# Rows beyond an expert's 96: blocks of 96 against blocks of 32, column-tiled and with the next block's transfers begun early

## The chip, the cores and the metric

One core of a Trainium2 chip runs the whole program in one launch. The metric is the device time of one launch in microseconds (us), as the median of three runs. TensorE, VectorE, ScalarE, GpSimd and SyncE are written PE, DVE, ACT, POOL and SP, as in the profile; a q behind the name (SPq, PEldq) is the engine's own sequencer with its branches, register operations and DMA issues.

## What is computed

The program is a small diffusion-like network (a gMLP layer, an RWKV layer, two attention layers) on 512 tokens and 256 context tokens of width 1024. Both of its first two layers end in a mixture of experts, which is where the change lies:

```python
def hier_moe(h, w_grp, b_grp, w_exp, b_exp, w_gate, w_up, w_down):
    ...
    expert_id = (grp[:, None] * EXPERTS_PER_GROUP + top_idx).reshape(-1)
    ...
    def expert_block(args):
        xb, e = args
        return (jax.nn.silu(xb @ w_gate[e]) * (xb @ w_up[e])) @ w_down[e]
    ...
    return jnp.einsum('tk,tkd->td', weights, y)
```

Each token is sent to 2 of 32 experts. In layer 0 there are 768 tokens (1536 rows over all experts), in layer 1 there are 512 (1024 rows). An expert has a gate and an up matrix of 1024 by 512 and a down matrix of 512 by 1024, all float32: 2 MB each, 6 MB an expert. Nothing bounds how many rows one expert gets. With the inputs that the reference draws, its router gives 114, 101 and 120 rows to the three busiest experts of layer 0 and 97 to the busiest of layer 1; all others have at most 96.

## The kernel before

`moe` runs five parts one after the other for each of the two layers: `norm_turn` (normalises the tokens, stores them in `h_rows`, and begins the loads of experts 0 and 1), `route`, `experts`, `experts_beyond`, `combine`. Each part is a block of its own, and all engines meet at its end; the helper `signals` then clears the semaphores in a short block of its own (L42, L46).

`route` works out on DVE which expert each row goes to and which place it has there. The first 96 rows (`CAP`) of an expert sit in the expert's own cell; rows above that go to further cells of 96. `index` holds for each cell the tokens of its rows, `home` for each token the rows of its results, `beyond` the number of further cells and the expert that owns each. All tables are as wide as the largest possible number of further cells, `blocks_beyond(nt)`: 16 in layer 0 and 10 in layer 1. L787 to L795 compare each count and place with the multiples of 96, L807 and L809 build the tables over all cells, L736 multiplies them on PE, L816 copies out the index.

`experts` goes through the 32 experts in a fixed, unrolled order. Weights sit in a ring of two (`wgu`, `wd`): SP fetches those of expert e+2 as soon as the sums of expert e are done. Each 96 rows are worked as 3 groups of 32; with 32 rows only a quarter of PE's columns is filled, so four quarters of the output columns are computed side by side on four column tiles (L886 gate and up, L904 down). Results leave in four stores by POOL (L866).

`experts_beyond` is a loop in hardware (`Fori`, L999) over all possible further cells, with an `If` (L1000) whose body runs for the cells that exist. A body is a block by itself:

```python
sp.dma_start(wgu[:, 0, 0, :, :], gate_src[bass.ds(e, 1)].rearrange("a p k f -> p (a k) f")).then_inc(gate_in, 16)
...
pool.indirect_dma_start(xs[:, :], None, h_rows, bass.IndirectOffsetOnAxis(ap=lanes[:, 0:1].bitcast(U32), axis=0)).then_inc(x_in, 16)
...
sp.wait_ge(y_ready, 2)
...
sp.wait_ge(y_out, 16)
```

SP issues gate, up and down weights (L1007 to L1009), POOL copies the cell's column of the index (L1016) and gathers the rows (L1018); PE turns them (L1024), multiplies all 96 rows at once with 512 columns (L1030), turns the hidden rows (L1034) and multiplies by the down matrix (L1040). DVE moves the turned rows (L1052) and the results (L1060), ACT applies silu (L1046). SP stores the results and waits until they have landed (L1011); then the block ends, the semaphores are cleared and the next turn of the loop begins.

`combine` gathers the two results of each token (L1086, POOL), loads the gate rows (L1078, SP) and adds into `x` on DVE (L1095 to L1098).

Of the kernel before, what the change touches and what calls it, by code (L numbers as in the profile page):

```python
# [7 lines left out]
P = 128  # L8
# [81 lines left out]
def constants():  # L90

    i, j = np.meshgrid(np.arange(P), np.arange(P), indexing="ij")
    return side_by_side({"ident": i == j, "before": i < j, "ones": np.ones((P, P)), "iota": np.tile(np.arange(P), (P, 1)),
                         "caps": np.tile(CAP * np.arange(1, 9), (P, 1)), "tokens": i[:, :NTA] + P * j[:, :NTA]})
# [26 lines left out]
def blocks_beyond(nt):  # L121

    return (2 * nt * P) // CAP
# [7 lines left out]
class Core:  # L131


    def __init__(self, nc, held, ins):
# [8 lines left out]
        self.y_rows = nc.dram_tensor("y_rows", [(E + blocks_beyond(NTA)) * CAP, D], F32, kind="Internal").ap()  # L143
# [500 lines left out]
def moe(core, layer, nt):  # L644
# [3 lines left out]
    nb = E + blocks_beyond(nt)  # L648
    with ExitStack() as held:
# [9 lines left out]
        beyond = sb("blocks_beyond", [P, blocks_beyond(nt) + 1], I32)  # L659
# [5 lines left out]
        gate_in, gate_in1, up_in, up_in1, down_in, down_in1, router_in, kept0, kept1 = held.enter_context(  # L665
            signals(nc, "gate_in0 gate_in1 up_in0 up_in1 down_in0 down_in1 router_in kept0 kept1"))
# [18 lines left out]
        experts(core, layer, h_rows, y_rows, index, wgu, wd, gate_src, up_src, down_src, gate_in, up_in, down_in)  # L685
        experts_beyond(core, layer, nt, h_rows, y_rows, index, beyond, wgu, wd, gate_src, up_src, down_src)
        combine(core, layer, nt, y_rows, weights, home)


def route(core, layer, nt, nb, br, kept, weights, index, home, beyond):  # L690
# [3 lines left out]
    more = -(-nt * P // CAP) - 1  # L694
    with ExitStack() as held:
# [17 lines left out]
        owner = sb("owner", [P, nbb, E])  # L713
# [6 lines left out]
        with nc.Block() as block:  # L720
# [26 lines left out]
            def _(dve):  # L747
# [49 lines left out]
                dve.tensor_scalar(first, blk, 1.0, None, ALU.min)  # L797
                do(dve.scalar_tensor_tensor(shift, shift, float(E - 1), iota[:, 0:E], ALU.add, ALU.subtract))
                dve.scalar_tensor_tensor(row, blk, float(-CAP), where, ALU.mult, ALU.add)
# [1960 lines left out]
```

## Time and profile before

| | |
|---|---|
| median of 3 runs | 4519.39 us (4518.64 to 4523.71) |
| the profiled execution | 4529.52 us, its span 4527.7 us |
| PE busy | 3775.3 us (83% of the span) |
| DVE, ACT, POOL busy | 1255.0, 777.2, 617.6 us |
| mean transfer rate | 154 GB/s |

The shares are means over very different stages. `experts` of layer 0 runs from about 747 to 1357 us, that of layer 1 from about 2969 to 3579 us; each is followed by `experts_beyond` and `combine`. "us" in a row is the start or the busy time as its view says; a row with three numbers and slashes gives the shortest, the median and the longest in ns.

### The profile page before, as it was taken

To read this page: it belongs to the slowest core of one execution; us is meant where nothing else is said; L and a number is where in the kernel's file an instruction comes from. 1 tells how busy PE (TensorE), PEld (TensorE's weight loads), DVE (VectorE), ACT (ScalarE), POOL (GpSimd) and SP (SyncE) were. 2 spreads that over 40 slices of the span, in tenths; PEclk is the share of its full clock that TensorE was granted. 3 is DMA by queue.
4 is the path that set the end of the run, shared out by engine and by line. 5 is a ranking of instruction groups with operands and counts; after the bars stand their busy time and mean duration, and the time that the engine had idled before them with its cause. 6 is when DMAs were issued, how large, how long until landed. Compare 5 with 4: busy or idle time off the path is not lost. (4 is left out here: it accounts for less than half of the span.)

```text
span 4527.7 us, 102783 instructions
## 1 busy us (share of the span) xinstructions
PE 3775.3 (83%) x45908; PEld 2400.6 (53%) x45908; DVE 1255.0 (28%) x2935; ACT 777.2 (17%) x1775; POOL 617.6 (14%) x792
## 2 busy tenths in 40 slices
PE   4999986999985289878888887789999739997787
PEld 2455535555552135467777775445555414564464
DVE  2140123111110530055545554421111120232153
ACT  1011001000000100133433331100000010231142
POOL 0000000111110100054444441011111010000000
PEclk7999996999997589889999997789999869758999
DMA  7731106999985332100000002279999633101100
GB/s 280 281 140 37 70 30 238 381 381 375 372 303 184 108 86 85 59 14 20 27 17 17 17 6 101 103 287 380 379 371 375 225 104 101 57 1 48 37 38 24
DMA packets 297853, 697.12 MB, mean 154 GB/s; under 512 B 26509, under 2 KB 49517, under 8 KB 296780
## 3 DMA queue, kind: packets, MB, share of 16 engines
q1 hardware_dynamic: 263268, 602.54, 37.0%
q0 software_dynamic: 26192, 73.25, 5.0%
q10 hardware_dynamic: 7960, 14.81, 0.9%
q8 instruction: 363, 5.95, 0.5%
q14 instruction: 70, 0.57, 0.0%
HBM read 636.40 MB, written 54.14 MB: 153 GB/s over the span
## 5 line engine op out<-in xcount | busy, mean ns | idle before, releaser
L886 PE MATMUL banks<-w_gate_up_ring,x_turned 128*32 128x256 f32 x12288 | 700.8, 384 | 63.5 <-DMA w_gate_up_ring<-in_moe_w_up_dram 62.0
L886 PEld LDWEIGHTS banks<-w_gate_up_ring,x_turned 128*32 128x32 f32 x12288 | 435.6, 111 | 302.7 <-issue 94.4
L904 PE MATMUL banks<-w_down_ring,hidden_turned 128*32 128x256 f32 x6144 | 344.8, 380 | 0.0
L962 DVE TENSOR_TENSOR hidden<-silu_gate,banks 128x128 f32<-128x128 f32 x192 | 55.3, 288 | 807.1 <-ACT silu_gate L942 807.1
L866 POOL DMA_DIRECT2D y_rows<-y_out_rows x256 | 141.0, 559 | 986.6 <-ACT y_out_rows L948 949.5
L904 PEld LDWEIGHTS banks<-w_down_ring,hidden_turned 128*32 128x32 f32 x6144 | 193.7, 110 | 128.0 <-issue 0.2
L337 PE MATMUL banks<-const_cols,h_tokens 128*128 128x128 f32 x240 | 55.0, 409 | 214.7 <-DVE h_tokens L310 143.6
L1883 DVE TENSOR_TENSOR inverse_both_ways<-banks,inverse_both_ways 128x512 f32<-128x512 f32 (+1 forms) x240 | 152.2, 637 | 255.3 <-PE banks L1792 254.4
L854 POOL DMA_INDIRECT x_rows<-h_rows,cell_index x64 | 62.7, 979 | 919.8 <-POOLq L42 893.6
L456 PE MATMUL banks<-gmlp_weights,h_turned_gmlp 128*128 128x512 f32 x384 | 173.3, 606 | 13.1 <-DMA gmlp_weights<-in_ga_w_in_dram 13.1
L1781 PE MATMUL banks<-inverse_both_ways,l_quarters 64*64 64x64 f32 x3840 | 150.7, 225 | 29.6 <-POOL inverse_both_ways L1965 21.7
L942 ACT ACTIVATE silu_gate<-banks 128x128 f32<-128x128 f32 x192 | 53.3, 278 | 711.0 <-PE banks L886 711.0
L630 PE MATMUL banks<-gmlp_weights,u_channels 128*128 128x512 f32 x384 | 165.1, 592 | 0.8 <-DVE u_channels L596 0.8
L487 PE MATMUL banks<-h_turned_gmlp,gmlp_weights 128*128 128x384 f32 x512 | 165.3, 486 | 0.0
L1300 PE MATMUL banks<-mixed,proj_weights 128*128 128x384 f32 x512 | 165.3, 486 | 0.0
L337 PEld LDWEIGHTS banks<-const_cols,h_tokens 128*128 128x128 f32 x240 | 45.7, 217 | 225.1 <-DVE h_tokens L310 151.6
L1781 PEld LDWEIGHTS banks<-inverse_both_ways,l_quarters 64*64 64x64 f32 x3840 | 130.7, 138 | 54.8 <-POOL inverse_both_ways L1965 24.6
L1792 PE MATMUL banks<-inverse_both_ways,step 64*64 64x64 f32 x3840 | 153.4, 220 | 0.3
L1911 ACT ACTIVATE step<-banks 128x256 f32<-128x256 f32 x240 | 92.2, 384 | 270.3 <-PE banks L1781 264.9
L1792 PEld LDWEIGHTS banks<-inverse_both_ways,step 64*64 64x64 f32 x3840 | 133.2, 137 | 3.2 <-ACT step L1911 2.6
L1300 PEld LDWEIGHTS banks<-mixed,proj_weights 128*128 128x128 f32 x512 | 97.3, 190 | 68.1 <-issue 0.5
L1970 POOL TENSOR_TENSOR l_quarters<-l_and_rb,scan_masks 128x256 f32<-128x256 f32 x192 | 123.5, 666 | 72.0 <-PE banks L1781 71.7
(452 smaller groups left out, 5530.1 us busy)
## 6 DMA issues: line engine op xcount, KB each, us to landing
w_gate_up_ring<-in_moe_w_gate_dram SPq DMA_DIRECT2D x68, 2048.0 KB, 20.7
w_gate_up_ring<-in_moe_w_up_dram SPq DMA_DIRECT2D x68, 2048.0 KB, 25.0
w_down_ring<-in_moe_w_down_dram SPq DMA_DIRECT2D x68, 2048.0 KB, 22.6
u_channels<-in_ada_w_dram SPq DMA_DIRECT2D x40, 1024.0 KB, 7.0
y_rows<-y_out_rows POOLq DMA_DIRECT2D x256, 96.0 KB, 5.4
gmlp_weights<-in_ga_w_in_dram SPq DMA_DIRECT2D x8, 2048.0 KB, 8.1
ab_weights<-in_ab_w_in_dram SPq DMA_DIRECT2D x6, 2048.0 KB, 8.6
ada_first<-in_ada_w_dram SPq DMA_DIRECT2D x2, 4096.0 KB, 18.3
```

The costliest lines, as they stand in the source:

```text
L337: last = pe.transpose(core.ps[:, 2 * (j % 2) + half, k * P:(k + 1) * P], h[:, j % 2, c0:c0 + P], core.c("ident"))
L456: last = pe.matmul(core.ps[:, step % 6, :], hT[:, k, t * P:(t + 1) * P], wring[:, i % 2, k, :], start=k == 0, stop=k == KD - 1)
L487: last = pe.matmul(core.ps[:, (step + 2) % 8, 0:TOK], wring[:, i % 2, k, m * P:(m + 1) * P], hT[:, k, half * TOK:(half + 1) * TOK], start= ...
L630: last = pe.matmul(core.ps[:, bank, :], uT[:, rest * KD + k, t * P:(t + 1) * P], wring[:, rest, k, :], start=rest == 0 and k == 0, stop=re ...
L866: pool.dma_start(y_blocks[e, j], ys[strip(j), r, :, :]).then_inc(y_out[r], 16)
L886: last = pe.matmul(ps[strip(j), GU + g, 0:2 * FQ].rearrange("p (a c) -> p a c", a=2), xT[:, e % 2, k, strip(g)], wgu[:, e % 2, :, k, j * F ...
L904: last = pe.matmul(ps[strip(j), Y + g // 2, (g % 2) * DQ:(g % 2 + 1) * DQ], hT[:, g, strip(k)], wd[:, e % 2, k, j * DQ:(j + 1) * DQ], star ...
L1300: last = pe.matmul(ps[:, i % 8, 0:HT2], wring[:, n % 2, k, m * P:(m + 1) * P], mix[:, j % 2, k, half * HT2:(half + 1) * HT2], start=k == 0 ...
L1781: last = pe.matmul(ps[row[cc], 4 * h + 1, u * CHUNK:(u + 1) * CHUNK], LQ[h][row[cc], n % 2, u, :], XX[h][row[cc], 0, u, :], start=True, st ...
L1792: last = pe.matmul(ps[row[cc], 4 * h, (4 + u) * CHUNK:(5 + u) * CHUNK], Z[h][row[cc], u, :], XX[h][row[cc], 1, u, :], start=True, stop=True)
L1883: DVE.mark(dve.tensor_tensor(x, ps[:, 4 * h, at], x, ALU.add), by_dve, f"XX{n}_{h}")
L1970: POOL.mark(pool.tensor_tensor(by_dir(LQ[h][:, n % 2, :, :]), by_dir(LR[h][:, :, 0, :]), quarters(n), ALU.mult), by_pool, f"LQ{n}_{h}")
```

## The change

- Rows beyond an expert's 96 are put in cells of 32 instead of 96. `blocks_beyond` becomes 2 * ceil((tokens - 96) / 32): 42 in layer 0 and 26 in layer 1, and the tables of `route` grow with it. `route` has three small DVE operations more, for places and result rows in cells of two sizes.
- A body of the loop now works 32 rows on four column tiles, as `experts` does: 32 products for gate and up together, one turn of the hidden rows, 16 products for down.
- The first further cell's rows and weights are fetched in `experts`: weights behind those of the last expert, the gather behind the stores of expert 30, into a tile of its own (`xb`). Each body then fetches the next cell's rows once its own are turned, and the next cell's weights once its own sums are done, into the same half of the ring. The semaphores of these loads (`next_gu`, `next_d`) live across bodies; SP passes them on to the body's own.
- The last body also begins a load, which no one uses; `combine` waits for it on SP.
- The results leave in four stores on ACT's queue instead of one on SP's, and ACT waits for them.

```diff
@@ -120,7 +120,7 @@
 
 def blocks_beyond(nt):
 
-    return (2 * nt * P) // CAP
+    return 2 * -(-(nt * P - CAP) // ROWS)
 
 
...
     tl = nt * P
-    nb = E + blocks_beyond(nt)
+    nb = E + blocks_beyond(nt) + 1
     with ExitStack() as held:
...
+        xb = sb("x_rows_beyond", [ROWS, D])
         gate_src = ins["moe_w_gate"][layer].rearrange("e (k p) f -> e p k f", p=P)
...
-            signals(nc, "gate_in0 gate_in1 up_in0 up_in1 down_in0 down_in1 router_in kept0 kept1"))
+        gate_in, gate_in1, up_in, up_in1, down_in, down_in1, router_in, kept0, kept1, next_gu, next_d = held.enter_context(
+            signals(nc, "gate_in0 gate_in1 up_in0 up_in1 down_in0 down_in1 router_in kept0 kept1 next_gu next_d"))
         gate_in, up_in, down_in = [gate_in, gate_in1], [up_in, up_in1], [down_in, down_in1]
 
         def loads(sp):
...
         lane_hot = sb("lane_hot", [P, 2 * nt, CAP])
         token_at = sb("token_at", [P, 2 * nt, nb])
-        owner = sb("owner", [P, nbb, E])
+        owner = sb("owner", [P, nbb + 1, E])
+        owners = sb("owners", [P, nbb + 1])
+        back = sb("rows_back", [P, 2 * nt])
...
                 dve.tensor_reduce(blk, past[:, :, :], AX, ALU.add)
                 do(dve.tensor_tensor(shift, whole, extra, ALU.subtract))
                 dve.tensor_scalar(first, blk, 1.0, None, ALU.min)
+                dve.scalar_tensor_tensor(row, blk, float(-ROWS), where, ALU.mult, ALU.add)
                 do(dve.scalar_tensor_tensor(shift, shift, float(E - 1), iota[:, 0:E], ALU.add, ALU.subtract))
-                dve.scalar_tensor_tensor(row, blk, float(-CAP), where, ALU.mult, ALU.add)
+                dve.scalar_tensor_tensor(row, first, float(ROWS - CAP), row, ALU.mult, ALU.add)
                 do(dve.tensor_tensor(work[:, :, :, :], one_hot[:, :, :, :], shift.unsqueeze(1).unsqueeze(1).to_broadcast([P, 2, nt, E]), ALU.mult))
                 do(dve.tensor_reduce(moved, work[:, :, :, :].rearrange("p a t e -> p (a t) e"), AX, ALU.add))
...
                 for n in range(2 * nt):
                     last = dve.tensor_scalar(token_at[:, n, :], iota[:, 0:nb], got[:, n:n + 1], tokens[:, n % nt:n % nt + 1], ALU.is_equal, ALU.mult)
                 last.then_inc(spread, 1)
-                dve.tensor_tensor(owner[:, :, :], whole.unsqueeze(1).to_broadcast([P, nbb, E]), iota[:, 0:nbb].unsqueeze(2).to_broadcast([P, nbb, E]), ALU.is_le)
+                dve.tensor_tensor(owner[:, :, :], whole.unsqueeze(1).to_broadcast([P, nbb + 1, E]), iota[:, 0:nbb + 1].unsqueeze(2).to_broadcast([P, nbb + 1, E]), ALU.is_le)
+                dve.scalar_tensor_tensor(back[:, :], got, float(-E), first, ALU.add, ALU.mult)
+                dve.tensor_copy(beyond[:, 0:1], whole[:, E - 1:E])
                 do(dve.scalar_tensor_tensor(row, got, float(CAP), row, ALU.mult, ALU.add))
+                dve.tensor_reduce(owners[:, :], owner[:, :, :], AX, ALU.add)
+                do(dve.scalar_tensor_tensor(row, back[:, :], float(ROWS - CAP), row, ALU.mult, ALU.add))
                 dve.tensor_copy(flat(home[:, :, :]), row)
-                dve.tensor_copy(beyond[:, 0:1], whole[:, E - 1:E])
-                do(dve.tensor_reduce(count[:, 3, 0:nbb], owner[:, :, :], AX, ALU.add))
-                dve.tensor_scalar(beyond[:, 1:nbb + 1], count[:, 3, 0:nbb], float(E - 1), None, ALU.min)
+                dve.tensor_scalar(beyond[:, 1:nbb + 2], owners[:, :], float(E - 1), None, ALU.min)
                 dve.wait_ge(tabled, 1)
                 dve.tensor_copy(index[:, :], core.ps[0:CAP, 2, 0:nb])
 
 
-def experts(core, layer, h_rows, y_rows, index, wgu, wd, gate_src, up_src, down_src, gate_in, up_in, down_in):
+def experts(core, layer, h_rows, y_rows, index, wgu, wd, gate_src, up_src, down_src, gate_in, up_in, down_in, beyond, xb, next_gu, next_d):
 
     nc = core.nc
     ps = core.ps
     X_LOW, X_HIGH, GU, H, Y = 0, 1, 2, 5, 6
...
@@ -847,6 +853,12 @@
                     sp.dma_start(wgu[:, r, 1, :, :], up_src[e]).then_inc(up_in[r], 16)
                     sp.wait_ge(y_sum, 2 * (e - 1))
                     sp.dma_start(wd[:, r, :, :], down_src[e]).then_inc(down_in[r], 16)
+                first = sp.value_load(beyond[0:1, 1:2], min_val=0, max_val=E - 1)
+                sp.wait_ge(gu_sum, GROUPS * (E - 1))
+                sp.dma_start(wgu[:, 0, 0, :, :], gate_src[bass.ds(first, 1)].rearrange("a p k f -> p (a k) f")).then_inc(next_gu, 16)
+                sp.dma_start(wgu[:, 0, 1, :, :], up_src[bass.ds(first, 1)].rearrange("a p k f -> p (a k) f")).then_inc(next_gu, 16)
+                sp.wait_ge(y_sum, 2 * (E - 1))
+                sp.dma_start(wd[:, 0, :, :], down_src[bass.ds(first, 1)].rearrange("a p k f -> p (a k) f")).then_inc(next_d, 16)
 
             @block.gpsimd
             def _(pool):
...
+                        pool.indirect_dma_start(xb[:, :], None, h_rows, bass.IndirectOffsetOnAxis(ap=index[0:ROWS, E:E + 1].bitcast(U32), axis=0)).then_inc(x_beyond, 16)
                 for r in range(2):
                     pool.wait_ge(y_out[r], 16 * QUARTERS * E // 2)
+                pool.wait_ge(x_beyond, 16)
 
             @block.tensor
             def _(pe):
...
-def experts_beyond(core, layer, nt, h_rows, y_rows, index, beyond, wgu, wd, gate_src, up_src, down_src):
+def experts_beyond(core, layer, nt, h_rows, y_rows, index, beyond, xb, next_gu, next_d, wgu, wd, gate_src, up_src, down_src):
...
+    X, GU, H, Y = 0, 1, 2, 3
+    QUARTERS = P // ROWS
+    FQ, DQ = F // QUARTERS, D // QUARTERS
+    strip = lambda j: slice(ROWS * j, ROWS * (j + 1))
+    y_blocks = y_rows[E * CAP:, :].rearrange("(b l) (q c) -> q l b c", l=ROWS, q=QUARTERS)
...
+        lanes = sb("lanes", [ROWS, 1], I32)
+        xT = sb("x_turned", [P, KD, ROWS])
+        sg = sb("silu_gate", [P, FQ])
+        h = sb("hidden", [P, FQ])
+        hT = sb("hidden_turned", [P, P])
+        ys = sb("y_out_rows", [P, DQ])
...
+        def block_beyond(b):
+            with signals(nc, "lanes_set x_in gu_here d_here x_turned x_moved gu_sum silu_done h_ready h_turned hT_ready y_sum y_ready y_stored", core.soft) as (
+                    lanes_set, x_in, gu_here, d_here, x_turned, x_moved, gu_sum, silu_done, h_ready, h_turned, hT_ready, y_sum, y_ready, y_stored):
+                with nc.Block() as block:
+                    @block.sync
+                    def _(sp):
+                        e = sp.value_load(beyond[0:1, bass.ds(b + 2, 1)], min_val=0, max_val=E - 1)
+                        sp.wait_ge(next_gu, 32)
+                        sp.sem_clear(next_gu)
+                        sp.sem_inc(gu_here, 1)
+                        sp.wait_ge(next_d, 16)
+                        sp.sem_clear(next_d)
+                        sp.sem_inc(d_here, 1)
+                        sp.wait_ge(gu_sum, 1)
+                        sp.dma_start(wgu[:, 0, 0, :, :], gate_src[bass.ds(e, 1)].rearrange("a p k f -> p (a k) f")).then_inc(next_gu, 16)
+                        sp.dma_start(wgu[:, 0, 1, :, :], up_src[bass.ds(e, 1)].rearrange("a p k f -> p (a k) f")).then_inc(next_gu, 16)
+                        sp.wait_ge(y_sum, 1)
+                        sp.dma_start(wd[:, 0, :, :], down_src[bass.ds(e, 1)].rearrange("a p k f -> p (a k) f")).then_inc(next_d, 16)
+
+                    @block.gpsimd
+                    def _(pool):
+                        pool.tensor_copy(lanes[:, :], index[0:ROWS, bass.ds(b + E + 1, 1)]).then_inc(lanes_set, 1)
+                        pool.wait_ge(lanes_set, 1)
+                        pool.wait_ge(x_turned, 1)
+                        pool.indirect_dma_start(xb[:, :], None, h_rows, bass.IndirectOffsetOnAxis(ap=lanes[:, 0:1].bitcast(U32), axis=0)).then_inc(x_in, 16)
+                        pool.wait_ge(x_in, 16)
+
+                    @block.tensor
+                    def _(pe):
+                        for k in range(KD):
+                            last = pe.transpose(ps[:, X, k * ROWS:(k + 1) * ROWS], xb[:, k * P:(k + 1) * P], core.c("ident", ROWS)[:, 0:ROWS])
+                        last.then_inc(x_turned, 1)
+                        pe.wait_ge(x_moved, 1)
+                        pe.wait_ge(gu_here, 1)
+                        for k in range(KD):
+                            for j in range(QUARTERS):
+                                last = pe.matmul(ps[strip(j), GU, 0:2 * FQ].rearrange("p (a c) -> p a c", a=2), xT[:, k, :],
+                                                 wgu[:, 0, :, k, j * FQ:(j + 1) * FQ], start=k == 0, stop=k == KD - 1)
+                        last.then_inc(gu_sum, 1)
+                        pe.wait_ge(h_ready, 1)
+                        pe.transpose(ps[:, H, 0:P], h[:, :], core.c("ident")).then_inc(h_turned, 1)
+                        pe.wait_ge(hT_ready, 1)
+                        pe.wait_ge(d_here, 1)
+                        for k in range(KF):
+                            for j in range(QUARTERS):
+                                last = pe.matmul(ps[strip(j), Y, 0:DQ], hT[:, strip(k)], wd[:, 0, k, j * DQ:(j + 1) * DQ], start=k == 0, stop=k == KF - 1)
+                        last.then_inc(y_sum, 1)
+
+                    @block.scalar
+                    def _(act):
+                        act.wait_ge(gu_sum, 1)
+                        act.activation(sg[:, :], ps[:, GU, 0:FQ], ACT.Silu).then_inc(silu_done, 1)
+                        act.wait_ge(y_ready, 1)
+                        for j in range(QUARTERS):
+                            act.dma_start(y_blocks[j][:, bass.ds(b, 1), :], ys[strip(j), :].unsqueeze(1)).then_inc(y_stored, 16)
+                        act.wait_ge(y_stored, 16 * QUARTERS)
+
+                    @block.vector
+                    def _(dve):
+                        dve.wait_ge(x_turned, 1)
+                        dve.tensor_copy(xT[:, :, :].rearrange("p k c -> p (k c)"), ps[:, X, 0:KD * ROWS]).then_inc(x_moved, 1)
+                        dve.wait_ge(silu_done, 1)
+                        dve.tensor_tensor(h[:, :], sg[:, :], ps[:, GU, FQ:2 * FQ], ALU.mult).then_inc(h_ready, 1)
+                        dve.wait_ge(h_turned, 1)
+                        dve.tensor_copy(hT[:, :], ps[:, H, 0:P]).then_inc(hT_ready, 1)
+                        dve.wait_ge(y_sum, 1)
+                        dve.tensor_copy(ys[:, :], ps[:, Y, 0:DQ]).then_inc(y_ready, 1)
+
         with nc.Fori(0, blocks_beyond(nt)) as b:
             with nc.If(left > b):
-                with signals(nc, "lanes_set x_in gate_in up_in down_in x_turned x_moved g_sum u_sum silu_done h_ready h_turned hT_ready y_sum y_ready y_out", core.soft) as (
...
+                block_beyond(b)
...
+                sp.wait_ge(next_gu, 32)
+                sp.wait_ge(next_d, 16)
```

## Rows read from the trace of the kernel before

**Rows 1.** Busy time by stretch: start and end, length, engines, granted clock, DMA share, GB/s.

```profile
811.00:1346.00 535.00, 500.58 (x8515) 310.65 (x8507) 77.15 (x229) 48.66 (x143) 88.64 (x140) 0.99 1.02 369
1361.70:1405.30 43.60, 25.70 (x60) 10.03 (x60) 3.63 (x6) 0.59 (x1) 1.16 (x2) 0.77 0.46 163
1489.00:1497.00 8.00, 0.00 (x0) 0.00 (x0) 0.00 (x0) 0.00 (x0) 0.24 (x1) 0.50 0.00 0
```

**Rows 2.** DMA issues: count, size, median us to landing.

```profile
y_rows<-y_out_rows_b SPq DMA_DIRECT2D x4, 384.0 KB, 3.0
```

**Rows 3.** Timeline of the three bodies of layer 0: start, us, engine, line, operation.

```profile
1352.53 2.16 POOL L866 DMA_DIRECT2D y_rows<-y_out_rows  x4 [15.22 <-ACT y_out_rows L948]
1361.72 0.18 POOL L1016 COPY lanes_b<-cell_index 96x1 int32 x1 [7.03 <-issue]
1362.81 0.40 SPq L1007 DMA_DIRECT2D w_gate_up_ring<-in_moe_w_gate_dram  x1
1370.39 1.54 PE L1024 MATMUL banks<-const_cols,x_rows_b 96*128 96x96 f32 x8 [18.89 <-DMA x_rows_b<-h_rows,lanes_b]
1373.79 16.50 PE L1030 MATMUL banks<-w_gate_up_ring,x_turned_b 128*96 128x512 f32 x32 [1.85 <-DMA w_gate_up_ring<-in_moe_w_gate_dram]
1392.34 7.11 PE L1040 MATMUL banks<-w_down_ring,hidden_turned_b 128*96 128x512 f32 x16 [0.65 <-DVE hidden_turned_b L1057]
1400.35 0.39 SPq L1011 DMA_DIRECT2D y_rows<-y_out_rows_b  x1
...
1405.33 0.18 POOL L1016 COPY lanes_b<-cell_index 96x1 int32 x1 [41.92 <-POOLq L42]
...
1485.71 0.37 SPq L1011 DMA_DIRECT2D y_rows<-y_out_rows_b  x1
```

**Rows 4.** Timeline of layer 1's only body and what follows.

```profile
3583.72 0.18 POOL L1016 COPY lanes_b<-cell_index 96x1 int32 x1 [6.97 <-POOLq L42]
...
3622.22 0.37 SPq L1011 DMA_DIRECT2D y_rows<-y_out_rows_b  x1
3631.34 0.83 SPq L1078 DMA_DIRECT2D gate_spread<-mods  x2
...
3640.20 0.75 DVE L1095 TENSOR_SCALAR y_back<-y_back,choice_weights 128x1024 f32<-128x1024 f32 x1 [18.15 <-DMA y_back<-y_rows,row_of_choice]
```

**Rows 5.** Timeline in `experts`: one group of 32 rows, then the down products of three.

```profile
1341.22 3.66 PE L886 MATMUL banks<-w_gate_up_ring,x_turned 128*32 128x256 f32 x64
...
1346.12 5.39 PE L904 MATMUL banks<-w_down_ring,hidden_turned 128*32 128x256 f32 x96
```

**Rows 6.** Landing after issue: up weights of L1008, then stores of L866.

```profile
DMA to landing us min/median/max: 15.0/15.5/16.7
...
DMA to landing us min/median/max: 2.1/5.4/7.2
```

**Rows 7.** Branches of the loop, L999, from the last body to `combine`: layer 0, then layer 1.

```profile
L999 SPq COMPARE_BRANCH  x27: 40/45/50, 1490.2 to 1498.7; - x27
L999 DVEq COMPARE_BRANCH  x27: 50/62/67, 1490.4 to 1499.8; - x27
L999 POOLq COMPARE_BRANCH  x27: 40/50/50, 1490.2 to 1496.0; - x27
L999 PEldq COMPARE_BRANCH  x27: 86/214/218, 1490.3 to 1500.0; - x27
L999 SPq COMPARE_BRANCH  x19: 40/50/60, 3626.7 to 3631.2; - x19
```

**Rows 8.** Timeline of the start of `combine` in layer 0.

```profile
1498.79 0.84 SPq L1078 DMA_DIRECT2D gate_spread<-mods  x2
1509.30 0.75 DVE L1095 TENSOR_SCALAR y_back<-y_back,choice_weights 128x1024 f32<-128x1024 f32 x1 [23.77 <-DMA gate_spread<-mods]
```

**Rows 9.** Timeline of `route` in layer 0: its tables.

```profile
739.98 0.68 DVE L809 TENSOR_TENSOR owner<-count,const_cols 128x512 f32<-128x512 f32 x1
744.22 0.20 DVE L816 CAST cell_index<-banks 96x48 int32<-96x48 f32 x1 [2.42 <-PE banks L736]
```

More of the change, by code:

```diff
@@ L93, in constants @@
     return side_by_side({"ident": i == j, "before": i < j, "ones": np.ones((P, P)), "iota": np.tile(np.arange(P), (P, 1)),
-                         "caps": np.tile(CAP * np.arange(1, 9), (P, 1)), "tokens": i[:, :NTA] + P * j[:, :NTA]})
+                         "caps": np.tile(CAP + ROWS * np.arange(21), (P, 1)), "tokens": i[:, :NTA] + P * j[:, :NTA]})
 def scan_constants():
@@ L658, in moe @@
         home = sb("row_of_choice", [P, 2, nt], U32)
-        beyond = sb("blocks_beyond", [P, blocks_beyond(nt) + 1], I32)
+        beyond = sb("blocks_beyond", [P, blocks_beyond(nt) + 2], I32)
+        xb = sb("x_rows_beyond", [ROWS, D])
         gate_src = ins["moe_w_gate"][layer].rearrange("e (k p) f -> e p k f", p=P)
@@ L684, in moe @@
         route(core, layer, nt, nb, br, [kept0, kept1], weights, index, home, beyond)
-        experts(core, layer, h_rows, y_rows, index, wgu, wd, gate_src, up_src, down_src, gate_in, up_in, down_in)
-        experts_beyond(core, layer, nt, h_rows, y_rows, index, beyond, wgu, wd, gate_src, up_src, down_src)
-        combine(core, layer, nt, y_rows, weights, home)
+        experts(core, layer, h_rows, y_rows, index, wgu, wd, gate_src, up_src, down_src, gate_in, up_in, down_in, beyond, xb, next_gu, next_d)
+        experts_beyond(core, layer, nt, h_rows, y_rows, index, beyond, xb, next_gu, next_d, wgu, wd, gate_src, up_src, down_src)
+        combine(core, layer, nt, y_rows, weights, home, next_gu, next_d)
 def route(core, layer, nt, nb, br, kept, weights, index, home, beyond):
@@ L693, in route @@
     nbb = blocks_beyond(nt)
-    more = -(-nt * P // CAP) - 1
+    more = nbb // 2
     with ExitStack() as held:
@@ L825, in experts @@
     FQ, DQ = F // QUARTERS, D // QUARTERS
-    y_blocks = y_rows.rearrange("(b g l) (q c) -> b q l g c", g=GROUPS, l=ROWS, q=QUARTERS)
+    y_blocks = y_rows[0:E * CAP, :].rearrange("(b g l) (q c) -> b q l g c", g=GROUPS, l=ROWS, q=QUARTERS)
     with ExitStack() as held:
@@ L834, in experts @@
         ys = sb("y_out_rows", [P, 2, GROUPS, DQ])
-        s = held.enter_context(signals(nc, "x_in0 x_in1 x_turned x_low x_high gu_sum silu_done h_ready h_turned hT_ready y_sum y_low y_high y_out0 y_out1", core.soft))
-        x_in0, x_in1, x_turned, x_low, x_high, gu_sum, silu_done, h_ready, h_turned, hT_ready, y_sum, y_low, y_high, y_out0, y_out1 = s
+        s = held.enter_context(signals(nc, "x_in0 x_in1 x_turned x_low x_high gu_sum silu_done h_ready h_turned hT_ready y_sum y_low y_high y_out0 y_out1 x_in", core.soft))
+        x_in0, x_in1, x_turned, x_low, x_high, gu_sum, silu_done, h_ready, h_turned, hT_ready, y_sum, y_low, y_high, y_out0, y_out1, x_beyond = s
         x_in, y_out = [x_in0, x_in1], [y_out0, y_out1]
@@ L989, in experts_beyond @@
     with ExitStack() as held:
         sb = lambda name, shape, dt=F32: held.enter_context(nc.sbuf_tensor(f"{name}_b{layer}", shape, dt))
-        lanes = sb("lanes", [CAP, 1], I32)
-        xs = sb("x_rows", [CAP, D])
-        xT = sb("x_turned", [P, KD, CAP])
-        sg = sb("silu_gate", [CAP, F])
-        h = sb("hidden", [CAP, F])
-        hT = sb("hidden_turned", [P, KF, CAP])
-        ys = sb("y_out_rows", [CAP, D])
-        left = nc.values_load(beyond[0:1, 0:1], min_val=0, max_val=blocks_beyond(nt))
+        lanes = sb("lanes", [ROWS, 1], I32)
@@ L1063, in combine @@
-def combine(core, layer, nt, y_rows, weights, home):
+                block_beyond(b)
+def combine(core, layer, nt, y_rows, weights, home, next_gu, next_d):
     nc = core.nc
```

59 lines of the change are left out of this document (2 added, 57 removed).

## The prediction

> **What bounds the kernel now.** I read the page's shares first (PE 83% busy, 154 GB/s on average) and then the busy time by stretch, because the mean says nothing about the stages that change. In `experts` PE runs at its upper clock level and the transfer engines are full, 369 GB/s [rows 1]: nothing is to be had there, and whatever is added to its traffic costs time. In a body of `experts_beyond` the picture is another: in 43.6 us PE is busy 25.7, the transfers run 46% of the time, one after the other [rows 1]. The count of result stores says how many bodies run: 4 in both layers together [rows 2]; the timeline puts three in layer 0 [rows 3] and one in layer 1 [rows 4].
>
> The timeline of a body shows why it is long. Weights are asked for at 1362.81, PE gets its rows at 1370.39 and its first weights at 1373.79; two products of 16.50 and 7.11 us follow; the store is issued at 1400.35 and the next body begins at 1405.33 [rows 3]. A store lands 3.0 us after its issue [rows 2], so 2.0 us of those 4.98 are the block's end, the clearing and the loop. Three bodies take from 1361.72 to the last landing at 1485.71 + 3.0 = 1488.7, 127.0 us; the one of layer 1 takes from 3583.72 to 3622.22 + 3.0 = 3625.2, 41.5 us.
>
> After the last body the loop goes on through its empty turns, 13 in layer 0 and 9 in layer 1. The branch rows give two branches a turn: SP (1498.7 - 1490.2) / 13 = 0.65 us, DVE 0.72, POOL 0.45, PE 0.75, and in layer 1 SP 4.5 / 9 = 0.50 [rows 7]. These turns are on the path: `combine` starts behind them.
>
> **How many bodies the new kernel runs.** Not the trace but the inputs decide this. The rows over 96 are 18, 5 and 24 in layer 0 and 1 in layer 1. Each is below 32, so three cells and one cell stay three and one.
>
> **A new body, step by step.** Let s be the moment when PE begins, about 0.3 us after POOL's copy of the index.
>
> 1. Rows are there already. Eight turns and one move of 256 columns. Before, eight turns of 96 rows took 1.54 us, and 3.4 us lay between their start and the first product, some of it a wait for weights [rows 3]. I take 1.8 (1.5 to 2.5).
> 2. Gate and up: 64 records, 3.66 us in `experts` [rows 5]. But PE has idled before, and the granted clock over a body is 0.77 against 0.99 [rows 1]. How much that costs: the 16 records of L1040 take 7.11 us, so 32 of L1030 would take 14.2 at the upper level, and took 16.50 [rows 3]. The 2.3 us lost mean some 4.6 us spent at 1.2 GHz instead of 2.4. Here that is most of the pass: 4.6 us do 2.3 us of work, the rest 1.4 us. That is 6.0, and 6.3 with the shorter warm-up before it (3.6 to 7.3). The sums are done at s + 8.1.
> 3. Silu, product, turn, move: between L1030's end and L1040's start lie 2.05 us with 512 columns [rows 3], in `experts` 1.24 between the last sums and the first down product, partly covered [rows 5]. I take 1.5.
> 4. Down: a third of 5.39 us [rows 5], 1.8 (to 3.6 at the lower level). s + 11.4.
> 5. Move of 256 columns 0.5; four issues on ACT: POOL's four took 2.16 us [rows 3], SP's single ones 0.39, so 2.0 (1.3 to 2.4).
> 6. Landing: stores that share the engines with weights took 2.1 to 7.2 us, 5.4 in the median [rows 6], those of the old body, alone, 3.0 [rows 2]. The next weights are in flight here, so 5.4. The results have landed at s + 19.3.
> 7. End, clearing, loop turn: 2.0 + 0.3. The next body begins at s + 21.6.
>
> The other bound of a body is the weights. SP can ask for the next 4 MB only at s + 8.1, because they go where the present ones lie. In the old body up landed 15.5 us after its issue, 16.4 after gate's, with down beside them [rows 6]; at the full 369 GB/s the 4.19 MB need 11.4. I take 14: they land at s + 22.3, and PE wants them at s + 21.6 + 1.8 = s + 23.4. That fits with 1 us to spare and fails by 1 us with 16.4, so I count 22 us from body to body. Down weights follow 6 us later and are wanted 8 us later. The gather is issued at about s + 1.5; before, 8.7 us lay between the copy of the index and PE's start on the gathered rows (1361.72 to 1370.39) [rows 3], so it arrives by s + 10 and is hidden by the same chain. SP waits inside its stream for the sums, but has nothing else behind them; ACT waits for its stores, with only the block's end behind.
>
> The first set of weights is asked for in `experts` one expert's time earlier than a body could. Before, the engines are idle for most of the last expert, so nothing there is delayed but the last four stores, issued at 1352.53 to 1354.7, whose landing may meet the last of 6 MB more. From there to the body lie 9.2 us [rows 3]. I add 1.5 us in each layer (0 to 3).
>
> Layer 0: two periods of 22 and 19.3 to the landing, 63.3 from s = 1362.0, so 1425.3 against 1488.7: -63.4. Layer 1: 3584.0 + 19.3 = 3603.3 against 3625.2: -21.9. Together -85.3, and +3 for the stores.
>
> **Empty turns.** There are 39 in layer 0 instead of 13, 25 in layer 1 instead of 9. Who comes to `combine` last matters. In layer 0 DVE began at 1509.30, when SP's gate rows had landed, 10.5 us after their issue and behind POOL's gathers [rows 8]; that is 19.2 us after the turns began. With 39 turns SP issues at 25.5; the gathers, begun at 39 x 0.45 = 17.4 plus 0.8, are then nearly over, so the gate rows land faster, within the 8.9 us that layer 1 shows for both kinds [rows 4]: 32 to 34 us, or +13 to +15. If SP's turn costs 0.50 as in layer 1, the gathers decide, +8. I take +11. In layer 1: 16 x 0.50 = +8 (7 to 10). Sum +19. PE's 39 x 0.75 = 29 us end inside `combine`, which has no work for it, and cost nothing. The unused load ends about 9 us after the last landing, before the gathers begin: nothing; if it were late, it would slow gathers that now take 8.9 us, by a few us at most.
>
> In the empty turns the transfer engines move nothing [rows 1], so this trace shows no instruction being fetched there. The Trainium skill, "Runtime: NRT & Kernel Launch", section "Instruction fetch mechanics", says that a taken branch whose target lies outside the fetched instructions waits for a fetch. That rule speaks against the change, which takes 42 more turns over a longer body; what it would do is the last rival below. The same skill's "Advanced Engine Details and Errata", section "Control Flow Timing", gives about 0.11 us for a compare-and-branch; by that an empty turn would be an estimated 0.2 us and the term +9 instead of +19. The rows decide for 0.45 to 0.75.
>
> **`route`.** Tables over 32 experts and the possible cells grow on DVE. L809 handles 512 elements in 0.68 us [rows 9], 1.3 ns each. Ahead of PE's product come 448 elements more in each of L787 and L790, 168 in each of L792 and L795, 324 in L807 and one operation: 2.2 us; in layer 1 776 elements and the operation, 1.2. The longer owner table (864 elements more, twice: 2.2 us) comes while DVE would wait 2.42 us for PE [rows 9]; without that wait it would cost those 2.2. I take +3 (2 to 6).
>
> **Sum.** -85.3 + 3 + 19 + 3 = -60.3. The terms come from the profiled execution, 4529.5 us with a span of 4527.7, 10 us above the median of 4519.4; stages this short scale by nothing worth counting. 4519.4 - 60.3 = 4459.
>
> **Rivals.**
>
> *The weights set the pace.* PE is at its upper level and the stores land in 2.1 us. Then a body's own chain is 1.8 + 3.6 + 1.5 + 1.8 + 0.5 + 1.3 + 2.1 = 12.6, and the cycle is 11.4 to 14 for the weights plus 3.9 for the next pass: 17. Layer 0 takes 34 + 12.6, 17 us less than counted, layer 1 7 less: 4435. For it: PE stays at the upper level through gaps of 2 us. Against it: each body has a gap of about 10 us.
>
> *Slow bodies.* Lower level throughout and late stores: 2.5 + 7.3 + 1.5 + 3.6 + 0.5 + 2.4 + 7.2 = 25.0, period 27.3. Layer 0 79.6 (+16), layer 1 +6: 4481. For it: the clock of 0.77 and stores behind 4 MB of weights.
>
> *One more cell.* If one expert had over 32 rows beyond, a body of 22 would replace an empty turn: 4480. 24 of 32 is the fullest, so it is unlikely; three more would take away all of the gain.
>
> *The turns eat the gain, slower than before.* One mechanism: a turn over the longer body waits for its instructions on each engine. With 64 empty turns the gain of 60 is gone when each costs 0.94 us more than the 0.5 to 0.65 counted, that is at about 1.6 us; at 2.5 us the kernel takes 64 x 2.5 - 38 = 122 us more, 4581. On PE alone it would decide later, since `combine` has no work for PE. Against it: the per-turn cost is as steady as a fixed number of instructions would be, and PE with the longest body is only 0.1 above SP.
>
> **Chances.** My forecast, 4445 to 4475, 0.62; weights set the pace 0.12; slow bodies 0.17; more cells 0.03; turns eat the gain 0.03; something else 0.03. The range of 4437 to 4488 leaves out the fastest half of the second case and the last ones. Differences within 0.2% (9 us) are about what a measurement of this kernel cannot tell from none. Only the turns' case ends on that side: faster 0.95, same 0.02, slower 0.03.
>
> **What would show it.** In the changed kernel: 6 loads of each weight beyond the 64 of the experts, 4 bodies; 21 to 23 us between two copies of the index; gate and up in about 6.3 us and then 1.8 for down; stores landing after about 5 us; 39 empty turns that take SP 20 to 25 us; DVE's first work in `combine` about 49 us earlier in layer 0 (-63.4 + 1.5 + 11 + 2), and 12 us closer to the end of `experts` in layer 1 (-21.9 + 1.5 + 8). I am wrong if a body waits on its weights for several us, if stores land later than 7 us, or if a turn costs over 1 us.

## The result, and the profile after

| | before | changed |
|---|---|---|
| median | 4521.55 us (4 runs) | 4424.22 us (4 runs, 4421.13 to 4436.23) |
| ratio | | 0.9781, 95% interval 0.9766 to 0.9795 |
| profiled execution | 4529.52 us | 4436.23 us |

The kernel is 97 us faster; 60 were forecast, and the range ended at 4437. The bodies are as forecast and a second gain of nearly 40 us, which the sum did not have, lies in `experts`, whose code did not change.

Busy time by stretch (start and end, length, engines, granted clock, DMA share, GB/s). The first row is a stretch inside `experts` of the kernel before; then come the same stretch of the changed kernel and two of its bodies:

```profile
811.00:1330.00 519.00, 485.33 (x8248) 301.89 (x8244) 75.19 (x223) 47.44 (x139) 86.47 (x136) 0.99 1.04 377
811.00:1330.00 519.00, 500.03 (x8581) 307.48 (x8577) 77.51 (x230) 48.69 (x143) 91.83 (x144) 1.00 1.04 391
1344.60:1365.00 20.40, 8.84 (x105) 4.50 (x105) 1.43 (x4) 0.28 (x1) 1.10 (x2) 0.75 0.62 215
1365.00:1384.80 19.80, 8.85 (x105) 4.51 (x105) 1.43 (x4) 0.28 (x1) 1.07 (x2) 0.76 0.86 316
```

A body shrank from 43.6 us [rows 1] to 20. The first two rows are the surprise: 391 GB/s, where the same stretch of the kernel before moved 377. `experts` of layer 0, from the first gather to the end of the last store's issue, took 608.1 us before and takes 588.6; layer 1 went from 608.4 to 590.4.

Timeline of the changed kernel, the end of `experts` and the first body of layer 0, against [rows 3]:

```profile
1335.10 2.20 POOL L878 DMA_DIRECT2D y_rows<-y_out_rows  x4 [14.01 <-ACT y_out_rows L963]
1344.66 0.18 POOL L1040 COPY lanes_b<-cell_index 32x1 int32 x1 [7.36 <-issue]
...
1344.77 1.05 PE L1049 MATMUL banks<-const_cols,x_rows_beyond 32*128 32x32 f32 x8 [10.71 <-PEq L42]
...
1346.34 5.53 PE L1055 MATMUL banks<-w_gate_up_ring,x_turned_b 128*32 128x256 f32 x64 [0.52 <-DVE x_turned_b L1079]
...
1352.59 0.52 SPq L1034 DMA_DIRECT2D w_gate_up_ring<-in_moe_w_up_dram  x1
...
1353.31 1.93 PE L1064 MATMUL banks<-w_down_ring,hidden_turned_b 128*32 128x256 f32 x32 [0.38 <-DVE hidden_turned_b L1083]
...
1355.93 1.83 ACTq L1073 DMA_DIRECT2D y_rows<-y_out_rows_b  x4
1365.03 0.18 POOL L1040 COPY lanes_b<-cell_index 32x1 int32 x1 [17.46 <-POOLq L42]
...
1366.81 1.51 PE L1055 MATMUL banks<-w_gate_up_ring,x_turned_b 128*32 128x256 f32 x12 [0.52 <-DVE x_turned_b L1079]
```

PE's first product now waits for DVE's move and for no transfer. The landings, us from issue, of the next up weights (L1034) and of the results (L1073), against [rows 6]:

```profile
DMA to landing us min/median/max: 13.4/13.5/13.5
...
DMA to landing us min/median/max: 4.8/5.1/5.7
```

Up weights issued at 1352.59 are there at 1366.1, and the next body's products want them at 1366.81. The chain of the body and the weights are 0.7 us apart.

Branches of the loop after the last body of layer 0, and the start of `combine`, against [rows 7, 8]:

```profile
L1087 POOLq COMPARE_BRANCH  x79: 40/45/50, 1404.7 to 1422.0; - x79
L1087 SPq COMPARE_BRANCH  x79: 40/45/50, 1404.8 to 1430.2; - x79
L1087 DVEq COMPARE_BRANCH  x79: 50/62/67, 1404.9 to 1433.1; - x79
L1087 PEldq COMPARE_BRANCH  x79: 86/214/218, 1404.9 to 1433.9; - x79
```

```profile
1437.35 0.75 DVE L1126 TENSOR_SCALAR y_back<-y_back,choice_weights 128x1024 f32<-128x1024 f32 x1 [41.00 <-DMA gate_spread<-mods]
```

39 turns: SP 25.4 / 39 = 0.65 us a turn, DVE 0.72, PE 0.74, POOL 0.44, all as before. DVE waits again for the gate rows, which SP could not ask for before 1430.3.

Where the profiled 93.3 us are, step by step; negative is time gained:

| step | forecast | layer 0 | layer 1 |
|---|---|---|---|
| `route` to the index copy or first gather | +3 for both | +2.1 | not taken apart |
| `experts` | 0 | -19.4 | -18.0 |
| last store's issue to first body | +1.5 each | +0.3 | +0.2 |
| bodies, to the first empty turn | -63.4, -21.9 | -68.3 | -23.2 |
| empty turns to DVE's first work in `combine` | +11, +8 | +13.4 | +11.4 |

The stretch between the layers, with layer 1's `route` in it, came out 1.8 us shorter. That makes -103. From DVE's first work in layer 1's `combine` to the end, 10 us were lost again in this execution, 9 of them in the last layer: there PE ran at a granted clock of 0.96 before and at 0.90 in the changed kernel, over the same 768 products. This is no cost of the change: that last part takes 887.5 us in the kernel before, 897.5 in this execution, and 887.6 and 887.0 in the profiled executions of e3 and e4 below, which run the same code there.

### The profile page after: what moved, and what is told of

It reads as the page before. It is cut to its first block and busy times, and to the rows that moved or that the text cites. A ratio compares the mean times of both kernels' runs of the same rounds, so it can differ in the third digit from the quotient of the medians.

```text
span 4434.4 us, 104053 instructions
## 1 busy us (share of the span) xinstructions
PE 3704.5 (84%) x46088; PEld 2369.3 (53%) x46088; DVE 1252.4 (28%) x2933; ACT 775.7 (17%) x1775; POOL 620.5 (14%) x794
## 5 line engine op out<-in xcount | busy, mean ns | idle before, releaser
L901 PEld LDWEIGHTS banks<-w_gate_up_ring,x_turned 128*32 128x32 f32 x12288 | 425.8, 110 | 275.6 <-issue 56.6
L866 POOL DMA_INDIRECT x_rows<-h_rows,cell_index x64 | 62.9, 983 | 921.0 <-POOLq L42 895.4
L957 ACT ACTIVATE silu_gate<-banks 128x128 f32<-128x128 f32 x192 | 53.3, 278 | 674.0 <-PE banks L901 674.0
L487 PEld LDWEIGHTS banks<-h_turned_gmlp,gmlp_weights 128*128 128x128 f32 x512 | 97.2, 190 | 67.6
## 6 DMA issues: line engine op xcount, KB each, us to landing
w_gate_up_ring<-in_moe_w_gate_dram SPq DMA_DIRECT2D x70, 2048.0 KB, 19.8
```

What stands on the lines that cost most here:

```text
L487: last = pe.matmul(core.ps[:, (step + 2) % 8, 0:TOK], wring[:, i % 2, k, m * P:(m + 1) * P], hT[:, k, half * TOK:(half + 1) * TOK], start= ...
L901: last = pe.matmul(ps[strip(j), GU + g, 0:2 * FQ].rearrange("p (a c) -> p a c", a=2), xT[:, e % 2, k, strip(g)], wgu[:, e % 2, :, k, j * F ...
```

## The experiments

What else differs in `experts`? Its instructions are the same, but its tiles lie elsewhere. The table of constants grew by 13 columns, and it stands ahead of all tiles of the layers in SBUF: everything behind it moved, and the ring of weights (`w_gate_up_ring`, `w_down_ring`) went from byte 43200 of each partition to byte 43264. In HBM, `y_rows` became shorter, and all internal tensors behind it moved. Theory 1 is the ring's place in SBUF; theory 2 is HBM; theory 3, taken up later, is the small tiles that moved with the ring. All medians of the kernel before in this section lie between 4522.2 and 4523.5 us.

**e1: the kernel before with the ring moved.**

```diff
-                         "caps": np.tile(CAP * np.arange(1, 9), (P, 1)), "tokens": i[:, :NTA] + P * j[:, :NTA]})
+                         "caps": np.tile(CAP * np.arange(1, 9), (P, 1)), "tokens": i[:, :NTA] + P * j[:, :NTA],
+                         "spare": np.zeros((P, 13))})
```

> The kernel before with 13 unused columns more in its table of constants, nothing else; the expert ring then begins at byte 43264 of each partition (a multiple of 128, as in the changed kernel) instead of 43200 (64 past one). Theory 1, the ring's place in SBUF makes the expert stages faster: each of the two takes 586 to 590 us instead of 606 to 608, the kernel is 35 to 40 us faster than before, and the rate in the stage goes from 377 to about 391 GB/s. Theory 2, the place of tensors in HBM or anything else in the change does it: no change (within 5 us of before).

Measured: 4481.41 us against 4522.16, ratio 0.9915 (0.9897 to 0.9933), 41 us faster. The expert stages take 589.2 and 585.1 us. One fact shown: 13 columns of zeros that nobody reads give the whole surprise. The rate in the stretch is 381 GB/s and not the 391 expected, but that is the window's doing: here the last weights have arrived before 1330 us, while the changed kernel goes on to fetch those of its first further cell. Up to 1310 us, when all three kernels still fetch, the kernel before moves 376 GB/s, the changed kernel 390, and e1:

```profile
811.00:1310.00 499.00, 480.17 (x8234) 297.95 (x8230) 73.94 (x219) 46.58 (x137) 88.03 (x139) 1.00 1.04 390
```

PE now waits for weights half as long. The groups of instructions of the page show this. The kernel before, then e1 (busy, mean ns; idle time before them and its cause):

```profile
L886 PE MATMUL banks<-w_gate_up_ring,x_turned 128*32 128x256 f32 x12288 | 700.8, 384 | 63.5 <-DMA w_gate_up_ring<-in_moe_w_up_dram 62.0
```

```profile
L887 PE MATMUL banks<-w_gate_up_ring,x_turned 128*32 128x256 f32 x12288 | 692.6, 381 | 31.1 <-DMA w_gate_up_ring<-in_moe_w_up_dram 28.8
```

The products take the same 0.38 us each. The two stages together became 42 us shorter in these executions. PE's wait for weights shrank by 33 of them, and the busy time of the products, which differs by 3 us even between before and e9 below, by 8. So it is mainly the transfer into the ring that became faster, and not PE's reading of it.

**e2: the changed kernel with the ring moved off again**, by 16 unused columns, to byte 43328.

```diff
+                         "spare": np.zeros((P, 16))})
```

> The changed kernel with 16 unused columns more in the table of constants, so that its ring begins at byte 43328, again 64 past a multiple of 128. Theory 1: the expert stages go back to 606 to 608 us each and the kernel is 35 to 40 us slower than the changed one, about 4461, which is what the prediction's sum gave. Theory 2: as the changed kernel, 4424.

Measured: 4465.3 us (4456.91 to 4470.98), ratio to before 0.9874 (0.9852 to 0.9896); 41 us slower than the changed kernel, expert stages of 609.5 and 609.4 us, and PE waits as before:

```profile
L902 PE MATMUL banks<-w_gate_up_ring,x_turned 128*32 128x256 f32 x12288 | 703.5, 385 | 63.6 <-DMA w_gate_up_ring<-in_moe_w_up_dram 61.9
```

This is what the change is worth by itself, 57 us of 4522, against a forecast of 60. With the ring at a good place in both kernels the difference is the same: e1's 4481.4 less the changed kernel's 4424.2 is 57 us too.

**e4: the changed kernel with HBM laid out as before.**

```diff
-        self.y_rows = nc.dram_tensor("y_rows", [E * CAP + blocks_beyond(NTA) * ROWS, D], F32, kind="Internal").ap()
+        self.y_rows = nc.dram_tensor("y_rows", [E * CAP + 48 * ROWS, D], F32, kind="Internal").ap()
```

> The changed kernel with y_rows as long as before (4608 rows instead of 4416), so that all tensors behind it in HBM lie where they lay before. Theory 1 (place in SBUF): no change from the changed kernel, 4424 within 5 us. Theory 2 (place in HBM): 35 to 40 us slower.

Measured: 4425.48 us, ratio 0.979 (0.9773 to 0.9807), expert stages 587.9 and 588.3: no difference from the changed kernel. Theory 2 falls.

**e5 and e6: which places are good ones.** The kernel before with 48 and with 82 unused columns; the ring begins at byte 43392 and 43520.

> The kernel before with 48 unused columns in the table of constants: the ring begins at byte 43392, a multiple of 128 but not of 256. If a start at a multiple of 128 is what counts: as e1, about 4481, expert stages of 588 to 590 us. If it takes a multiple of 256: as before, 4522, 608 us a stage.

> The kernel before with 82 unused columns: the ring begins at byte 43520, a multiple of 512. If a multiple of 128 is enough, as e1 and e5, about 4481. If coarser places give more still: expert stages shorter than 588 us; but PE alone needs 17.4 us an expert, 32 of them and the first fill about 580, so at most 10 us a stage and 20 us in all.

Measured: e5 4522.58 us, ratio 0.9995 (0.9985 to 1.0005), stages 606.1 and 606.0; e6 4480.16 us, ratio 0.99 (0.988 to 0.992), stages 588.9 and 587.8. My guess of 128 was wrong: a multiple of 128 is no help, a multiple of 256 is, and 512 adds nothing.

**e9: the small tiles moved, the ring not.**

```diff
         wd = sb("w_down_ring", [P, 2, KF, D])
+        pad = sb("spare", [P, 16])
```

> The kernel before with 64 unused bytes behind the ring: the ring stays at byte 43200, while the index, the gathered rows, their turned copies and the results of the expert stages lie exactly where e1 had them. If the ring's own place is the cause: as before, 4522, 606 to 608 us an expert stage. If the places of the small tiles (gathers into them, stores out of them) are: as e1, 4481.

Measured: 4521.54 us, ratio 1.0002 (0.999 to 1.0014), stages 608.8 and 606.8; PE's products take 697.9 us and wait 64.2 for the up weights, as before. Theory 3 falls, and the ring's own place is left. Which of its two tiles counts, gate and up or down, was not tried.

**e3: what the empty turns cost.** The changed kernel with a shorter loop, 16 and 10 turns; it leaves out any cell beyond those, and with these inputs there is none.

```diff
-        with nc.Fori(0, blocks_beyond(nt)) as b:
+        with nc.Fori(0, 16 if nt == NTA else 10) as b:
```

> The changed kernel with its loop over possible cells cut to 16 turns in layer 0 and 10 in layer 1 (cells beyond those would not be worked; with these inputs there are none). If the empty turns cost what the trace of the changed kernel says (from the end of the last body to DVE's first work 13.5 us more than before in layer 0 and 11.4 us more in layer 1), the kernel is about 25 us faster than the changed one, 4399. If combine would hide them, under 5 us.

Measured: 4396.72 us, ratio to before 0.9727 (0.971 to 0.9745), 27.5 us faster than the changed kernel. From the first copy of the index to DVE's first work in `combine` it takes 77.9 us instead of 92.7 in layer 0 and 34.9 instead of 44.6 in layer 1, 24.5 together. SP's 0.65 and 0.64 us for the 26 and 16 turns left out would be 27, so the turns are on the path at very nearly their full price.

**e7: no weights ahead of time.** The changed kernel, with each body asking for its own weights when it starts.

```diff
-                first = sp.value_load(beyond[0:1, 1:2], min_val=0, max_val=E - 1)
-                sp.wait_ge(gu_sum, GROUPS * (E - 1))
-                sp.dma_start(wgu[:, 0, 0, :, :], gate_src[bass.ds(first, 1)].rearrange("a p k f -> p (a k) f")).then_inc(next_gu, 16)
...
-                        e = sp.value_load(beyond[0:1, bass.ds(b + 2, 1)], min_val=0, max_val=E - 1)
+                        e = sp.value_load(beyond[0:1, bass.ds(b + 1, 1)], min_val=0, max_val=E - 1)
+                        sp.dma_start(wgu[:, 0, 0, :, :], gate_src[bass.ds(e, 1)].rearrange("a p k f -> p (a k) f")).then_inc(next_gu, 16)
...
+                        sp.dma_start(wd[:, 0, :, :], down_src[bass.ds(e, 1)].rearrange("a p k f -> p (a k) f")).then_inc(next_d, 16)
                         sp.wait_ge(next_gu, 32)
```

> The changed kernel, but each body asks for its own weights at its own start, none is asked for in experts and none for the next; rows are still gathered ahead. My sum: gate and up land 13.5 to 16 us after the body's start, then 4 to 6 us of products, 1.5, 1.9, 0.5, 1.8 and 3 to 5 us of landing, 2 us to the next: 30 to 34 us a body instead of 20; 4 bodies, 40 to 56 us, less 1 to 2 us because nothing is left in flight: 4464 to 4480. The rest of the gain on a body (from 43 to about 31) is then the smaller block and its column tiles. Rival: the weights were never what a body waits for, and the body stays at 20 to 23 us: under 4436.

Measured: 4461.31 us, ratio to before 0.9867 (0.9847 to 0.9887), 37 us slower than the changed kernel, just under the expected 40 to 56. Its timeline of PE:

```profile
1343.69 1.05 PE L1041 MATMUL banks<-const_cols,x_rows_beyond 32*128 32x32 f32 x8 [10.75 <-PEq L42]
1359.36 5.55 PE L1047 MATMUL banks<-w_gate_up_ring,x_turned_b 128*32 128x256 f32 x64 [14.62 <-SPq L1024]
...
1366.34 1.93 PE L1056 MATMUL banks<-w_down_ring,hidden_turned_b 128*32 128x256 f32 x32 [0.39 <-DVE hidden_turned_b L1075]
1374.02 1.05 PE L1041 MATMUL banks<-const_cols,x_rows_beyond 32*128 32x32 f32 x8 [5.75 <-PEq L42]
```

A body takes 30.3 us, with 14.6 between the turns of the rows and the gate and up products, where the changed kernel has 0.5; the difference is the wait for weights. With 42 to 44 us before and 20 in the changed kernel, about 12 of the 22 us gained per body come with the smaller block, its column tiles and the rows gathered ahead, and 10 with the weights fetched ahead. Between the down products and the next body lie 4.2 us less: 1368.27 to 1374.02 is 5.8 us, in the changed kernel 1355.24 to 1365.24 is 10.0. Most of that is the landing of the four stores, 1.5 us here with no weights in flight and 5.1 in the changed kernel with the next weights beside them. Fetching ahead thus takes back 3.6 us a body of what it gives.

**e8: the turns skipped in groups**, for any input. The loop of the changed kernel in two levels:

```diff
-        with nc.Fori(0, blocks_beyond(nt)) as b:
-            with nc.If(left > b):
-                block_beyond(b)
+        INNER = 7 if nt == NTA else 13
+        with nc.Fori(0, blocks_beyond(nt) // INNER) as o:
+            with nc.If(left > o * INNER):
+                with nc.Fori(0, INNER) as i:
+                    with nc.If(left > o * INNER + i):
+                        block_beyond(o * INNER + i)
```

> The changed kernel with its loop in two levels, so that whole groups of empty cells are skipped by one branch: 6 outer turns of 7 in layer 0 and 2 of 13 in layer 1, and the same work for any input. Turns: after 3 bodies 4 empty inner and 5 outer ones instead of 39 in layer 0; 12 and 1 instead of 25 in layer 1. At 0.65 and 0.55 us a turn 30 x 0.65 + 12 x 0.55 = 26 us fewer: about 4398. If the outer level costs a fetch of instructions each time or its registers slow each turn: 4405 to 4424.

Measured: 4402.79 us, ratio to before 0.973 (0.9711 to 0.9749), 21 us faster than the changed kernel. The two levels are worth 21 us where 26 were expected, less than the cut loop of e3 gives but with nothing left out. SP's branches of the two levels, outer and inner, after the last body of layer 0:

```profile
L1088 SPq COMPARE_BRANCH  x11: 40/50/53, 1411.2 to 1415.1; - x11
...
L1090 SPq COMPARE_BRANCH  x9: 45/50/58, 1408.8 to 1411.0; - x9
```

6.3 us in place of 25.4. An outer turn costs SP (1415.1 - 1411.2) / 5 = 0.8 us. From the first copy to DVE the stretch is 77.1 us in layer 0 instead of 92.7 and 39.2 instead of 44.6 in layer 1; the coarse grouping of layer 1 leaves 12 inner turns.

**e10: e8 with `combine`'s gate rows loaded earlier**, at the end of `experts` and no longer in `combine`.

```diff
...
+                for st in range(2):
+                    ap, at = mod_row(core, layer, st, 5)
+                    sp.dma_start(gt[:, st, :], rows(ap, at, D)).then_inc(gates_in, 16)
...
```

> e8 with combine's two gate rows loaded at the end of experts instead of in combine. In e8 DVE begins 9.3 us after POOL's first gather in layer 0 and 8.5 in layer 1, in the changed kernel 14.5 and 9.3. If the gathers alone take 8.9 us (as before's layer 1), this gives 0 to 2 us beside e8: 4400 to 4403. If the gate rows' 1 MB slows the gathers that run beside it, they land sooner without it and it gives up to 3 us a layer: down to 4396.

Measured: 4408.78 us (4400.06 to 4414.6), ratio to before 0.9755 (0.9738 to 0.9772), no gain over e8, where 4396 to 4403 had been expected. From the first copy to DVE it does gain 3.4 us in layer 0 (73.6) and 1.9 in layer 1 (37.3), but from the end of the last store's issue in `experts` to that copy it takes 9.6 and 10.9 us, against 7.8 and 8.1 in e8. That pays back 4.6 of the 5.3 us; what lengthened the stretch was not taken apart. Its runs spread over 14 us, so a small loss against e8 is not shown either.

## Why the prediction was wrong

**The step that failed** is the first one: "In `experts` PE runs at its upper clock level and the transfer engines are full, 369 GB/s [rows 1]: nothing is to be had there, and whatever is added to its traffic costs time." Full engines were taken for a fixed rate. The 369 itself was low, because the row of the prediction reaches to 1346 us, past the end of the last weights; up to 1330 it was 377. The busy share of the transfer engines is 1.04 at 377 GB/s and 1.04 at 391: it says that they had work, not how fast the work went. The stage was bound by its transfers, which the prediction saw, so a transfer that goes faster was worth having: 4% more rate gave about 19 us a layer. The change got it by accident, with 13 more columns in a table ahead of the ring. The longer table of the cells' multiples is one line of the full diff (`CAP + ROWS * np.arange(21)` for `CAP * np.arange(1, 9)`), which the excerpt above leaves out; the prediction priced its comparisons on DVE and never asked what its columns push along. e1, e2, e5, e6 and e9 show this in both directions: over all runs, with the ring at a multiple of 256 bytes a stage takes 585 to 591 us, at 64, 128 or 192 past one 606 to 610.

The Trainium skill, "DMA: Bandwidth & Descriptors", section "How a descriptor splits into AXI transactions", has a rule that fits: a transfer is cut into transactions of 256 bytes that begin at multiples of 256, so a piece that does not begin there starts with a transaction that fetches bytes no one uses. Each row of weights here is 2048 or 4096 bytes, so off such a place it would need one transaction more. The section speaks of what a transaction reads; here it is the written side that moved, which it does not mention. The runs agree with the place (256, neither 128 nor 512). They do not show the growth with the offset that the section's beats imply: 64, 128 and 192 bytes past cost about the same. No run here looks inside a packet, so that this is the mechanism is argued from the page, and only the dependence on the place is shown.

**The rest, by its own steps.** The sum without that gain was 4459; e2, which is the change without it, took 4465.

1. Four bodies, as the counts of rows said: 70 loads of each weight, 64 + 4 + 2 unused. Right.
2. Turns and move 1.57 us for 1.8; gate and up 5.53 for 6.3; to the down products 1.44 for 1.5; down 1.93 for 1.8; four issues 1.83 for 2.0; landing 4.8 to 5.7 for 5.4. Period 20.4 and 19.8 us for 22. The largest miss is the slow part of gate and up: the pass is 3.66 us at the upper level, so 1.9 us were lost to the lower one where 2.3 to 2.6 had been counted. This differs between executions: in e2, with the same code, the four passes took 6.0 to 6.6 us and the period in layer 0 was 20.9.
3. The weights almost set the pace: 14 us for 4 MB was 13.5 plus the 0.5 between the two issues. The two bounds lie 0.7 us apart where 1.1 had been forecast, and in e2 0.1: up weights issued at 1376.48 landed 13.7 us later, at 1390.2, and the products began at 1390.28.
4. Empty turns: +24.8 for +19. In layer 0 the price a turn was right and the landing of the gate rows was right to 1 us; I had then taken 11 from a span of 8 to 15, and it was 13.4. In layer 1, SP's turn cost (3527.9 - 3512.0) / 25 = 0.64 us and POOL's 0.59, where the kernel before had 0.50 and 0.42. The price of a turn is thus not a property of the loop alone. The rival in which the turns eat the whole gain needed 1.6 us and is far off; from 1412 to 1422 us, inside the empty turns, the transfer engines moved nothing, so no fetch of instructions is visible there. e3 measured 27.5 for the 42 turns it left out. By the Trainium skill, "Advanced Engine Details and Errata", section "Control Flow Timing", the estimate for the term was +9; the trace gives +24.8, and it decides.
5. Stores of the last expert: +0.3 and +0.2 for +1.5 each, though +1.2 and +1.4 in e2; `route` in layer 0 +2.1 for about 2.2, the owner table hidden by DVE's wait, which fell from 2.42 us [rows 9] to 0.48.

In the changed kernel's trace the misses of the bodies and of the empty turns cancel nearly: -6.2 and +5.8. In e2's trace the two together, from the first copy of the index to DVE's first work in `combine`, came to -53.3 us in layer 0 and -10.9 in layer 1, for -52.4 and -13.9 forecast. That the sum without the ring's place came out within 6 us is partly luck.

## What to carry to other kernels

Where a stage is bound by its transfers, write down where its tiles begin in SBUF, before and after a change, and let them begin at multiples of 256 bytes; a table made longer anywhere ahead of them can move the time nearly as much as the change itself, here 41 us beside 57. A loop over the largest possible count pays for every empty turn on every engine, here 0.45 to 0.75 us each and 64 times, and a second level that skips groups gets most of it back. Fetching ahead was worth 10 us of a 30 us body. A shorter chain in the body would probably gain little more by itself, though no run tried it: the weights, 13.5 us from issue to landing, are there only 0.1 to 0.7 us before they are wanted.

## What the runs showed of the hardware

- The ring's first byte alone decides the rate in `experts`: 376 to 377 GB/s, with PE waiting 59 to 64 us for the up weights over both stages, or 390 to 392 GB/s, with 29 to 32 us of waiting. 43264 and 43520 are good, 43200, 43328 and 43392 bad. The whole program moves by 0.9%.
- A busy share of the transfer engines at or above 1.0 does not mean that their rate cannot rise: it was 1.04 at 377 GB/s and at 391.
- The four 32 KB stores of a body landed 1.5 us after their issue with nothing beside them (e7) and 5.1 us after it with 6 MB of weights in flight.
- An empty turn of a hardware loop, the same few register operations and branches, cost SP 0.50 us in one place of a program and 0.64 to 0.65 in others, POOL 0.42 to 0.59, DVE 0.53 to 0.72, and was steady within one loop: in the changed kernel's layer 0 SP took 15 or 16 branches in each 5 us. What in the place decides this is open; it was not tried.
